# Order of weight copies, merged tiles, residual and context norm in a fused two-block kernel

## The reference

```
proj   = einsum('bsnc,ncd->bsnd', branches, w_o_branch[l])
gates  = sigmoid(merge.reshape(B, S, 4, D) + b_gate[l])
merged = sum(gates * proj, axis=2)
x      = layer_norm(ALPHA * x + merged @ w_out[l], ln_g[l], ln_b[l])
```

## Time and profile before

| | us |
|---|---|
| median of 3 runs | 3420.7 (3420.3 to 3421.48) |
| the profiled execution | 3420.07 |
| its span | 3418.3 |
| TensorE busy | 3225.6 (94%) |
| DVE busy | 1500.7 (44%) |
| ACT busy | 1188.0 (35%) |
| POOL busy | 1488.2 (44%) |

### The profile page before, as it was taken

The page is one execution under the profiler, slowest core; times in us unless marked ns, Lnnn a source line. Parts: engine busy times, 40 slices in busy tenths (PEclk is TensorE's granted clock), DMA queues, the critical chain, the costliest instruction groups (busy, mean ns, idle before and its releaser), DMA issues. The chain is left out here.

```text
span 3418.3 us, 51762 instructions
## 1 busy us (share of the span) xinstructions
PE 3225.6 (94%) x21116; PEld 2532.1 (74%) x21116; DVE 1500.7 (44%) x2378; ACT 1188.0 (35%) x1940; POOL 1488.2 (44%) x820
## 2 busy tenths in 40 slices
PE   8899998999898999989998988999999989899999
PEld 6784786788577747867886756888888876678787
DVE  6633374898666333848896236210000022520000
ACT  6234433422362334343223435322112233532221
POOL 4431553454344225534552258333334433845454
PEclk9999999999999999999999999999999999999999
...
DMA packets 77611, 284.18 MB, mean 83 GB/s; under 512 B 8736, under 2 KB 8736, under 8 KB 76864
## 3 DMA queue, kind: packets, MB, share of 16 engines
...
## 5 line engine op out<-in xcount | busy, mean ns | idle before, releaser
L131 POOL TENSOR_TENSOR lows<-ring,highs 128x1024 fp32r<-128x1024 f32 x376 | 939.1, 2498 | 1607.3 <-ACT highs L123 1590.4
L155 PE MATMUL ps<-x_high,highs 128*128 128x512 f32 x1936 | 771.6, 399 | 36.2 <-ACT highs L123 17.4
L158 PE MATMUL ps<-x_low,highs 128*128 128x512 f32 x1936 | 758.7, 392 | 0.0
L123 ACT ACTIVATE highs<-ring 128x1024 fp32r<-128x1024 f32 x376 | 396.9, 1056 | 749.9 <-PE ps L155 388.4
L155 PEld LDWEIGHTS ps<-x_high,highs 128*128 128x128 f32 x1936 | 366.2, 189 | 127.1 <-issue 30.7
L158 PEld LDWEIGHTS ps<-x_low,highs 128*128 128x128 f32 x1936 | 365.9, 189 | 78.3 <-issue 3.5
L2744 DVE TENSOR_TENSOR hidden_scratch<-ps,hidden_scratch 128x512 f32<-128x512 f32 x44 | 30.4, 692 | 546.0 <-PE ps L2063 541.5
L677 PE MATMUL ps<-x_high,lows 128*128 128x512 f32 x1040 | 256.8, 389 | 0.0
L677 PEld LDWEIGHTS ps<-x_high,lows 128*128 128x128 f32 x1040 | 195.3, 188 | 40.5
L2620 DVE SCALAR_TENSOR_TENSOR BR<-ps,mod,BR 128x512 f32<-128x512 f32 x72 | 47.4, 662 | 368.8 <-PE ps L167 368.8
L167 PE MATMUL ps<-hidden_parts,lows 128*128 128x512 f32 (+1 forms) x528 | 188.8, 358 | 0.0
...
## 6 DMA issues: line engine op xcount, KB each, us to landing
ring<-in_w SPq DMA_DIRECT2D x414, 512.0 KB, 3.5
merging<-in_ada SPq DMA_DIRECT2D x48, 512.0 KB, 3.5
BR<-in_ada SPq DMA_DIRECT2D x48, 512.0 KB, 3.5
X<-in_xT SPq DMA_DIRECT2D x4, 512.0 KB, 6.7
...
merging<-in_cond SPq DMA_DIRECT2D x4, 512.0 KB, 4.7
...
```

Source lines behind the costliest of these rows:

```text
L123: nc.scalar.activation(self.high(n), self.chunk(n), ACT.Copy).then_inc(self.hi_made, 1)
L131: nc.gpsimd.tensor_tensor(self.low(n), self.chunk(n), self.high(n).bitcast(F32), ALU.subtract).then_inc(self.lo_made, 1)
L155: mm = nc.tensor.matmul(ps, high, xhigh, start=start, stop=False)
L158: nc.tensor.matmul(ps, high, xlow, start=False, stop=False)
```

## The change

- The high copy of the next stage's first chunk moves: in the latent projections from behind the last value eviction to behind the first of four; in the gates and memory stage from behind the two value evictions to ahead of them.
- Merged tiles: MH and ML are allocated for the merging stage as well. Tile m is copied and subtracted there while tile m + 1 is merged, for m = 0 to 6. At the end of the merging stage PE makes the high-part products of the first two output tiles for k = 0 to 6. The output stage splits tile 7 alone.
- For that the merging stage's memory is laid out anew in BR: MG has two slots, GATE three, WEIGHTED one, three row buffers. The conditioning vectors and row groups 1 and 2 are transferred only after branch splits; the reductions are spread over gates 0 to 28 and written straight into `mods`.
- The residual: DVE adds x_high and x_low ahead of the wait for the product, then one operation makes `alpha * x + product`. RUN holds seven rows; the output stage's last matmul multiplies ones by RUN, and the next stage adds the eighth row in the same bank.
- The context's transfer no longer waits for the fourth merged split; its norm and subtractions are made one output tile sooner.
- In the recurrence PE does k = 0 and 1 of the first tile before it waits for the second chunk's high copy.

```diff
@@ -525,7 +525,7 @@
             S = self.S
-            nc.tensor.matmul(PS[:, 6, :], C("ones", P), self.run, start=True, stop=True).then_inc(S("sum"), 1)
+            nc.tensor.matmul(PS[:, 6, :], C("ones", P), self.rows[:, 7, :], start=False, stop=True, skip_group_check=True).then_inc(S("sum"), 1)
@@ -715,12 +715,11 @@
                 before.tensor(pe)
-            for j in range(2):
-                stream.wait_high(pe, n0 + j)
-            for k in range(DK):
+            for j, k in [(j, k) for ks in ((0, 1), *((k,) for k in range(2, DK))) for j in range(2) for k in ks]:
+                if k == 0:
+                    stream.wait_high(pe, n0 + j)
                 pe.wait_ge(before.S("x_low"), k + 1)
-                for j in range(2):
-                    with_high(nc, PS[:, j, :], tile_of(stream.high(n0 + j), k), XH[:, k, :], XL[:, k, :], k == 0)
+                with_high(nc, PS[:, j, :], tile_of(stream.high(n0 + j), k), XH[:, k, :], XL[:, k, :], k == 0)
@@ -1380,9 +1379,10 @@
                 for q in range(4):
+                    if q == 1:
+                        stream.hi(nc, act, n0 + 11 + 1)
...
                     a.activation(VV[:, q, :], PS[:, q % 2, :], ACT.Copy).then_inc(S("v_out"), 1)
-                stream.hi(nc, act, n0 + 11 + 1)
@@ -1533,10 +1533,10 @@
                     a.activation(BR[:, 8 + c, :], Y0[:, c, :], ACT.Silu, scale=par_col("cln_g", c), bias=par_col("cln_b", c)).then_inc(S("branch"), 1)
+                stream.hi(nc, act, nm + 8 + 1)
...
                     a.activation(VX[:, q, :], PS[:, 4 + q, :], ACT.Copy).then_inc(S("value_out"), 1)
-                stream.hi(nc, act, nm + 8 + 1)
@@ -1597,37 +1597,41 @@
         BL, BH = (room.enter_context(nc.sbuf_tensor(f"branches_{part}{layer}", [P, NB * WT, T], F32R))[:, :, :] for part in ("low", "high"))
-        Y = room.enter_context(nc.sbuf_tensor(f"merging{layer}", [P, 18 * T], F32))
...
-        GATE, WEIGHTED, MG = YT(0, 4), YT(4, 4), BR[:, 0:8, :]
-        AD = WEIGHTED[:, 0, 0:96].rearrange("p (m c) -> p m c", c=2)
-        PROD, CB = Y[:, 8 * T:10 * T], Y[:, 10 * T:14 * T].rearrange("p (c k) -> p c k", c=2)
+        Y = room.enter_context(nc.sbuf_tensor(f"merging{layer}", [P, 2 * T], F32))
+        kept = ExitStack()
+        MH, ML = (kept.enter_context(nc.sbuf_tensor(f"merged_{part}{layer}", [P, DK, T], F32R, side="right"))[:, :, :] for part in ("high", "low"))
...
+        CB, GATE, WEIGHTED = flat(0, 4).rearrange("p (c k) -> p c k", c=2), BR[:, 4:7, :], BR[:, 7, :]
+        MG, PROD = BR[:, 8:10, :], flat(10, 2)
+        AD = mods[:, layer, :].rearrange("p (m c) -> p m c", c=2)
+        ROWS = (Y[:, :], flat(12, 2), flat(14, 2))
...
         def rows_of(t):
-            s = t % 4
-            return Y[:, (14 + 2 * s) * T:(16 + 2 * s) * T] if s < 2 else BR[:, 4 + 2 * s:6 + 2 * s, :].rearrange("p a t -> p (a t)")
+            return ROWS[t % 3]
...
             def _(sp):
+                stream.send(sp, n0 + RING)
+                clear(sp, other)
+                sp.dma_start(rows_of(0), A["ada"][layer, 0, :, :]).then_inc(S("rows0"), 16)
+                sp.wait_ge(S("branch_low"), 4)
...
                     sp.dma_start(CB[:, c, :], A["cond"][c].partition_broadcast(P)).then_inc(S("cond"), 16)
-                stream.send(sp, n0 + RING)
-                clear(sp, other)
-                for t in range(48):
+                for t in range(1, 48):
                     stream.send(sp, n0 + RING + 45 * t // 48)
-                    if t >= 4:
-                        sp.wait_ge(S("ada"), 2 * (t - 3))
-                    elif t >= 2:
-                        sp.wait_ge(S("branch_low"), 4 + 4 * t)
-                    sp.dma_start(rows_of(t), A["ada"][layer, t, :, :]).then_inc(S(f"rows{t % 4}"), 16)
+                    if t < 3:
+                        sp.wait_ge(S("branch_low"), 12 + 2 * t)
+                    else:
+                        sp.wait_ge(S("ada"), 2 * (t - 2))
+                    sp.dma_start(rows_of(t), A["ada"][layer, t, :, :]).then_inc(S(f"rows{t % 3}"), 16)
@@ -1653,6 +1657,12 @@
                             mm.then_inc(S("product"), 1)
+                for t in range(2):
+                    pe.wait_ge(S("gate"), 29 + t)
+                    stream.wait_high(pe, n0 + 48 + t)
+                    for k in range(7):
+                        pe.wait_ge(S("merged_low"), k + 1)
+                        with_high(nc, PS[:, t, :], tile_of(stream.high(n0 + 48 + t), k), MH[:, k, :], ML[:, k, :], k == 0, used if t == 0 and k == 0 else None)
@@ -1664,15 +1674,21 @@
                     act.wait_ge(S("gate_product"), i + 1)
-                    if i >= 4:
-                        act.wait_ge(S("weighted"), i - 3)
-                    nc.scalar.activation(GATE[:, i % 4, :], PS[:, i % 4, :], ACT.Sigmoid, bias=par_col("b_gate", 8 * (i % 4) + i // 4)).then_inc(S("gate"), 1)
+                    if i >= 3:
+                        act.wait_ge(S("weighted"), i - 2)
+                    else:
+                        act.wait_ge(S("branch_low"), 5 + i)
+                    nc.scalar.activation(GATE[:, i % 3, :], PS[:, i % 4, :], ACT.Sigmoid, bias=par_col("b_gate", 8 * (i % 4) + i // 4)).then_inc(S("gate"), 1)
                     stream.hi(nc, act, min(gate_chunk(i) + (4 if i % 2 else 3), n0 + 48 + 1))
+                    if i >= 4 and i % 4 == 0:
+                        act.wait_ge(S("merged"), 3 * i // 4)
+                        nc.scalar.activation(MH[:, i // 4 - 1, :], MG[:, (i // 4 - 1) % 2, :], ACT.Copy).then_inc(S("merged_high"), 1)
...
                         nc.scalar.activation(CB, CB, ACT.Silu).then_inc(S("silu_c"), 1)
+                stream.hi(nc, act, n0 + 48 + 2)
@@ -1684,25 +1700,25 @@
                     dve.wait_ge(S("product"), i + 1)
-                    dst = MG[:, m, :] if n == 0 else WEIGHTED[:, n, :]
-                    if i >= 4 and n:
-                        dve.wait_ge(S("merged"), 3 * m - 3 + n)
-                    v.tensor_tensor(dst, PS[:, 4 + i % 4, :], GATE[:, i % 4, :], ALU.mult).then_inc(S("weighted"), 1)
+                    if i == 0:
+                        dve.wait_ge(S("branch_low"), 16)
+                    if n:
+                        dve.wait_ge(S("merged"), 3 * m + n - 1)
+                    v.tensor_tensor(WEIGHTED if n else MG[:, m % 2, :], PS[:, 4 + i % 4, :], GATE[:, i % 3, :], ALU.mult).then_inc(S("weighted"), 1)
...
                         dve.wait_ge(S("weighted"), i + 1)
-                        if n > 1:
-                            dve.wait_ge(S("merged"), 3 * m + n - 1)
-                        v.tensor_tensor(MG[:, m, :], MG[:, m, :], WEIGHTED[:, n, :], ALU.add).then_inc(S("merged"), 1)
+                        v.tensor_tensor(MG[:, m % 2, :], MG[:, m % 2, :], WEIGHTED, ALU.add).then_inc(S("merged"), 1)
...
                         dve.wait_ge(S("silu_c"), 1)
-                    for t in range(min(48, 48 * i // 30), min(48, 48 * (i + 1) // 30)):
-                        dve.wait_ge(S(f"rows{t % 4}"), 16 * (t // 4 + 1))
+                    if i >= 5 and n == 1:
+                        dve.wait_ge(S("merged_high"), m)
+                        v.tensor_tensor(ML[:, m - 1, :], MG[:, (m - 1) % 2, :], MH[:, m - 1, :].bitcast(F32), ALU.subtract).then_inc(S("merged_low"), 1)
+                    for t in range(min(48, 48 * i // 29), min(48, 48 * (i + 1) // 29)):
+                        dve.wait_ge(S(f"rows{t % 3}"), 16 * (t // 3 + 1))
...
                             v.tensor_tensor_reduce(PROD, rows_of(t), CB[:, c, :], 1.0, 0.0, ALU.mult, ALU.add, AD[:, t, c:c + 1]).then_inc(S("ada"), 1)
-                dve.wait_ge(S("ada"), 96)
-                v.tensor_copy(mods[:, layer, :], WEIGHTED[:, 0, 0:96]).then_inc(S("mods"), 1)
@@ -1711,17 +1727,17 @@
         if layer == 0:
...
-    MH, ML = (room.enter_context(nc.sbuf_tensor(f"merged_{part}{layer}", [P, DK, T], F32R))[:, :, :] for part in ("high", "low"))
-    MG, RR, RUN = BR[:, 0:8, :], BR[:, 8:16, :], BR[:, 7, :]
...
+    RR, RUN = BR[:, 8:16, :], BR[:, 7, :]
@@ -1741,14 +1757,12 @@
                     pe.wait_ge(S("residual"), t - 3)
-                if t == 0:
-                    stream.wait_high(pe, n0)
+                if t < 2:
+                    pe.wait_ge(S("merged_low"), 1)
+                    with_high(nc, PS[:, t, :], tile_of(stream.high(n0 + t), 7), MH[:, 7, :], ML[:, 7, :], False, stream.used if t else None)
+                    stream.wait_split(pe, n0 + t)
                     for k in range(DK):
-                        pe.wait_ge(S("merged_low"), k + 1)
-                        with_high(nc, PS[:, 0, :], tile_of(stream.high(n0), k), MH[:, k, :], ML[:, k, :], k == 0, stream.used if k == 0 else None)
-                    stream.wait_split(pe, n0)
-                    for k in range(DK):
-                        mm = nc.tensor.matmul(PS[:, 0, :], tile_of(stream.low(n0), k), MH[:, k, :], start=False, stop=(k == DK - 1))
```

(29 more changed lines are left out.)

25 lines of the change are left out of this document (13 added, 12 removed).

## The result

Five runs of the changed kernel took 3400.2 to 3407.33 us, median 3403.95; the kernel before, run beside it, 3420.94. The ratio is 0.9948 [0.9937, 0.9959]: 17 us faster, where 38 were forecast. The profiled execution took 3407.33 (span 3405.5), the longest of the five, 12.7 us under the profiled one of before.

What follows compares the result with a forecast made beforehand. TensorE, busy 3225.6 of 3418.3 us, bounds the kernel; only its pauses and low clock can pay. Terms 6.9 + 5.5 + 6.1 + 12.8 - 4 + 3.0 + 5.7 + 1.7 = 37.7 us gave 3383 us, range 3370 to 3402.

Steps and rivals of the forecast that it cites:

- Copies ahead of the last values: Attention entries, both layers: pauses shorter by 6.9 us (latent) and 6.1 (memory), plus 5.5 from the clock behind latent entries.
- Merged tiles split early: Merging stage's end into output stage: 28 of 48 matmuls run early, 3.4 us pause remains; 6.4 us gained per layer, 12.8 together.
- The 3.4 us of low clock: Behind the merged-split pause and possibly at the merging stage's start: 3.4 us at half clock, costing 1.7 us.
- Residual and mean: First output stage's end: residual in one operation and mean by a second matmul shorten the pause and keep the clock; 3.0 us.
- Program start: Start of program, layer 0: four matmuls of the first chunk run before the second chunk's high copy; 1.7 us gained.
- Context norm: Second output stage: norm a tile sooner removes a 1.39 us wait and brings TensorE back sooner; 5.7 us gained.
- The start of the merging stage is worse: Merging stage's start: fourth weight chunk's transfer stands behind branch-split waits on SyncE; 2 us lost per layer, 4 in all.
- I count 0; bounds 0 and 5 us for both layers together: Inside the merging stages: added copies, subtractions and fewer slots cost TensorE nothing; bounds 0 and 5 us.
- The cover: Merging stage: distance from a product to where its lateness reaches TensorE; sigmoid and weight copy by 14.3 us, wanted at 16.8.
- The modulation rows have three buffers instead of four: Merging stage: listed among what the split adds, with the rows ending one gate sooner; counted within the 0 us.
- C: Full merging tiles: VectorE or ScalarE late with the new single slots; some 15 us lost, 3398; chance 8%.
- D: Merging stage: merged tile's copy on ScalarE waits for VectorE ahead of the next weight copy; costs 42 us, 3425; chance 4%.

Runs made afterwards that it cites:

- experiment 5: Kernel before, with only the two moved weight copies (ahead of the last memory-attention values and of both latent values): 3409.58 us, 0.9963.
- experiment 3: Changed kernel without modulation row transfers after the third; VectorE does all its operations on the first three rows, modulation wrong: 3388.72 us, 0.9900.
- experiment 4: Changed kernel with four row buffers, the sums' unread product overlaid in bfloat16 on the weighted tile (the overlay): 3396.6 us, 0.9924.
- experiment 6: Changed kernel with four row buffers and two weight chunks sent before row waits: 3392.0; plus gate tiles over branches 0 to 2: 3392.3; plus later merged copies: 3400.32 us.
- experiment 7: On experiment 6's last kernel, cumulatively: seventh copy back at gate 28, 3397.08; weight sends a row sooner, 3396.69; GpSimdE's copy ahead of the barrier, 3391.87 us.
- experiment 8: Experiment 7's third kernel with the seventh copy at gate 29: 3398.89 us; its second with each row's second sum over 64 of 1024 columns: 3383.53 us.
- experiment 1: Changed kernel with the early split taken out, merging stage and eight merged copies as before: 3395.23 us, 0.9924.

## Why the prediction was wrong

By its own steps:

- **Copies ahead of the last values**: right in all three terms where they were to show, 6.96 for 6.9, 6.15 for 6.1, and 5.24 for the 5.5 of the clock. Alone, though, the copies brought 11 us and not 18.5 (experiment 5).
- **Merged tiles split early**: the mechanism was right to the pause (3.23 and 3.22 us for 3.4, VectorE's split caught, 2.23 for 2.4), the size 14.8 for 12.8. The 3.4 us of low clock that this term and that of the merging stage's start count stood in no row; behind this pause the changed kernel's matmuls are 0.43 us apart until about 881.3, some 4 us.
- **Residual and mean**: 3.86 up to the next layer's first matmul for 3.0; 1.1 of it is lost again in that layer's first pair, at the lower clock. **Program start**: 1.25 for 1.7. **Context norm**: the wait of 1.39 is gone, and from the last product to the squares 4.57 us are saved, in the pause, in the mean and, 1.84 of them, in the sixteen matmuls behind it; together 6.0 for 5.7.
- **"The start of the merging stage is worse", 4 us**: the place was right, and the size wrong: the steps at chunk 3 and behind it are 3.9 and 5.7. The term counted the late transfer, at 0.3 to 1.2 us, and took ScalarE to be in time; the gate tiles' place over branch 4 (1.3 us of ScalarE) was not in it, and the pauses were 3.15 and 4.76. Up to chunk 3 the growth of layer 0 is 5.5, because the stage also begins at the lower clock: its first matmuls are 0.43 us apart until 591.2, where before they were 0.23 apart, 1.6 us. That is luck of the run: five of the experiments' traces have it in layer 0 too, and the others not.
- **"I count 0; bounds 0 and 5 us for both layers together"** is the step that failed: the stages grew by another 6.8 and 3.6 us, 10.4 together, behind chunk 3. The cover was reckoned from VectorE through the sigmoid to the weight copy, 16.8 us, and that chain was not the one that broke: in the changed kernel's trace TensorE waits, above all before chunk 18, for high copies whose *transfer* is late. The way that decides goes from VectorE's sums through a row buffer to SyncE, where the next weight stands behind the row. "The modulation rows have three buffers instead of four" was named and priced at nothing; it should have been read in SyncE's order, where a row that waits for one buffer more holds a weight whose own slot is free. Experiments 3 and 4 show it by taking the waits away from either side, the one by leaving the rows out and the other by the fourth buffer.
- **Rivals.** C ("VectorE or ScalarE late in the full tiles", 15 us, 3398) came nearest in time, and its mechanism is what lies below the queue: experiments 4, 6, 7 and 8 show it at 4.7 to 8.0 us a layer in kernels with the queue mended and the overlay in place. In experiment 3, with no waits for rows and no overlay, it does not appear. D's copy that holds ScalarE for VectorE is real, up to 12.2 us, at a price of 7 to 8 us a layer in the worst variant and not 21. VectorE's window of 32.40 of 33 us was on the page: I took the other tiles' 3 to 6 idle us as reserve. From 800 to 850 us VectorE was busy for 41.02 us before and is for 48.74 in the changed kernel.
- **The second block** was no term. Of the 25 us between the forecast and the profiled run, the merging stages make 17.6, and 7.3 stand in the second block, in matmuls that the edit leaves as they were; the rest cancels.

The best versions found are those of experiments 6 (both queue edits, 0.9918 [0.9905, 0.9932]) and 7 (0.9914 [0.9900, 0.9928]): faster than the changed kernel, whose interval begins at 0.9937. They can't be told from experiment 1, which drops the split altogether, 0.9924 [0.9910, 0.9937]: no run shows that the early split is worth anything in the end. What also remains open is how much of the 17 us is the clock's luck: the runs of one and the same edited kernel differ by 4 to 12 us, those of the kernel before mostly by 4, with a few 5 to 10 us longer.
